# Retention's rotation moved from TensorE to copies within SBUF, in a stack of four mixed layers

## The reference, cut to what matters

```python
def _rotary(t, positions):
    half = t.shape[-1] // 2
    freq = ROPE_BASE ** (-jnp.arange(half, dtype=jnp.float32) / half)
    ang = positions.astype(jnp.float32)[..., None] * freq
    cos = jnp.cos(ang)[:, :, None, :]
    sin = jnp.sin(ang)[:, :, None, :]
    t1 = t[..., :half].astype(jnp.float32)
    t2 = t[..., half:].astype(jnp.float32)
    return jnp.concatenate([t1 * cos - t2 * sin, t1 * sin + t2 * cos], axis=-1).astype(t.dtype)
...
def _layer(x, c, positions, norm_g, w_ada, b_ada, w_in, conv_w, conv_b,
           dt_bias, a_log, d_skip, ssd_norm_g, b_forget, w_out):
...
    ret = _retention(rq.reshape(b, L, RET_HEADS, RET_HEAD_DIM),
                     rk.reshape(b, L, RET_HEADS, RET_HEAD_DIM),
                     rv.reshape(b, L, RET_HEADS, RET_HEAD_DIM), positions)
    ret = ret.reshape(b, L, RET_WIDTH) * jax.nn.silu(rg)
...
    mixed = jnp.concatenate([ret.astype(x.dtype), ssd.astype(x.dtype), fox.astype(x.dtype)], axis=-1)
    out = mixed @ w_out
    return x + gate[:, None, :] * out
```

## Time and profile before

| | us |
|---|---|
| median of 3 runs | 3217.77 (3216.93 to 3218.05) |
| the profiled execution: its own time | 3218.23 |
| its span | 3216.4 |
| TensorE busy | 3149.3 (98%) |
| VectorE busy | 1725.1 (54%) |
| ScalarE busy | 1205.2 (37%) |
| GpSimd busy | 446.8 (14%) |

### The profile page before, as it was taken

One profiled execution on the slowest core, in us unless ns is written; L12 is line 12 of the kernel. 1 busy time (PEld: TensorE's weight loads), 2 busy tenths in 40 slices (PEclk: granted clock), 3 DMA queues, 4 the chain that ended last, 5 costly groups with the idle time before them and its releaser, 6 DMA issues.

```text
span 3216.4 us, 43798 instructions
## 1 busy us (share of the span) xinstructions
PE 3149.3 (98%) x18127; PEld 2503.1 (78%) x18127; DVE 1725.1 (54%) x2545; ACT 1205.2 (37%) x1919; POOL 446.8 (14%) x359
## 2 busy tenths in 40 slices
PE   8999999999999999999999999999999999999999
PEld 6776778876777888887777788888888887778887
DVE  7965456845456443347877544345464334553333
ACT  4355434535542322233344432223352224342221
POOL 0022012003000310112322021011011001011110
PEclk9999999999999999999999999999999999999999
DMA  6764233336331233342100133333223322023332
GB/s 240 243 189 139 66 105 122 121 109 175 91 105 59 93 98 98 99 121 92 60 2 2 47 114 106 94 97 98 89 91 96 99 87 81 8 89 98 99 95 82
DMA packets 103654, 321.60 MB, mean 100 GB/s; under 512 B 10657, under 2 KB 26273, under 8 KB 101281
## 3 DMA queue, kind: packets, MB, share of 16 engines
q1 hardware_dynamic: 98128, 296.77, 29.8%
q10 hardware_dynamic: 5328, 22.02, 2.1%
HBM read 309.05 MB, written 9.70 MB: 99 GB/s over the span
## 4 chain that ended last, share of the span: by engine, by line
PE 86%; DVE 4%; ACT 2%; issue 1%; POOL 1%; DMA 0%; SPq 0%; DVEq 0%; POOLq 0%; ACTq 0%
PE acc L497 71%; PE acc L2553 1%; PE acc L1540 1%; PE acc L2539 1%; PE aux L1838 1%; PE aux L3334 1%; PE aux L1852 1%; PE acc L1865 1%; PE acc L2040 1%; PE aux L2029 1%; ACT w_hi L401 1%; PE aux L3339 1%; DVE ssd_ex L1429 0%; PE acc L3373 0%; DVE w_lo L408 0%
## 5 line engine op out<-in xcount | busy, mean ns | idle before, releaser
L497 PE MATMUL acc<-op_hi,w_hi 128*128 128x512 f32 x2624 | 1072.1, 409 | 7.4 <-DVE op_lo L1176 3.9
L401 ACT ACTIVATE w_hi<-raw 128x1024 fp32r<-128x1024 f32 (+2 forms) x476 | 494.1, 1038 | 1487.6 <-PE acc L497 1477.4
L497 PE MATMUL acc<-op_lo,w_hi 128*128 128x512 f32 x2624 | 1026.7, 391 | 0.0
L497 PE MATMUL acc<-op_hi,w_lo 128*128 128x512 f32 x2624 | 1026.3, 391 | 0.0
L408 DVE TENSOR_TENSOR w_lo<-raw,w_hi 128x1024 fp32r<-128x1024 f32 (+2 forms) x476 | 579.2, 1217 | 252.7 <-ACT w_hi L401 252.2
L497 PEld LDWEIGHTS acc<-op_hi,w_hi 128*128 128x128 f32 x2624 | 494.3, 188 | 136.8 <-issue 35.0
L497 PEld LDWEIGHTS acc<-op_lo,w_hi 128*128 128x128 f32 x2624 | 494.8, 189 | 106.2 <-issue 9.8
L497 PEld LDWEIGHTS acc<-op_hi,w_lo 128*128 128x128 f32 x2624 | 494.1, 188 | 105.3
L497 PE MATMUL acc<-ffn_hi,w_hi 128*128 128x512 f32 x800 | 311.8, 390 | 0.0
L497 PE MATMUL acc<-ffn_hi,w_lo 128*128 128x512 f32 x800 | 311.6, 390 | 0.0
L497 PE MATMUL acc<-ffn_lo,w_hi 128*128 128x512 f32 x800 | 311.6, 389 | 0.0
(11 more groups left out here) (592 smaller groups left out, 3574.2 us busy)
## 6 DMA issues: line engine op xcount, KB each, us to landing
raw<-in_w SPq DMA_DIRECT2D x436, 512.0 KB, 3.6
late_ada<-in_ada ACTq DMA_DIRECT2D x32, 512.0 KB, 4.5
raw<-in_w SPq DMA_DIRECT2D x32, 384.0 KB, 2.9
ssd_ex<-cum SPq DMA_DIRECT2D x16, 512.0 KB, 5.4
ssd_ex<-cum SPq DMA_DIRECT2D x16, 384.0 KB, 6.4
ada<-in_ada ACTq DMA_DIRECT2D x4, 1024.0 KB, 14.5
ada<-in_ada SPq DMA_DIRECT2D x4, 1024.0 KB, 21.8
ssd_ex<-cum SPq DMA_DIRECT2D x16, 256.0 KB, 4.8
```

The source lines that it names most:

```text
L401: act.activation(self.w_hi[g % AHEAD][:, 0:k, :], self.raw[s][:, 0:k, :], ACT.Copy).then_inc(self.split_hi.handle, 1)
L497: mm = pe.matmul(self.bank(s, g), w[:, k, :], a[:, k, 0:s.n], start=(k == 0 and q == 0), stop=(k == k_tiles - 1 and q == 2))
```

## The change

The product with `rot` is taken off TensorE. SyncE copies the two halves of the partitions of a tile, swapped, into one of four buffers (`swaps`, at the place of the forgetting attention's v, which is read by then). The sign goes into the sines: in the startup the sine's angle is multiplied by -1 on the lower half of the partitions (`half_sign`, in place of `rot` in the constant table). GpSimd multiplies the tile by the cosines in place, VectorE the swapped copy by the sines in place, and then adds the copy to the tile. The rotation no longer waits for the end of the forgetting attention, only for its transposes of v; its first copy is due 33 units before `start` (and no earlier than two units after the begin of retention's v pieces), the following ones 3.4 units apart. From the fifth copy on, a copy waits until the add has freed its buffer.

```diff
@@ -123,10 +123,7 @@
-    rot = np.zeros((P, P))
-    rot[i[:HD] + HD, i[:HD]] = -1.0
-    rot[i[:HD], i[:HD] + HD] = 1.0
-    parts["rot"] = rot
+    parts["half_sign"] = np.where(i < HD, -1.0, 1.0)[:, None]
@@ -970,7 +967,7 @@
-                act.activation(dst[:, :], dst[:, :], ACT.Sin).then_inc(*self.sined.inc())
+                act.activation(dst[:, :], dst[:, :], ACT.Sin, scale=1.0 if i else core.c("half_sign")).then_inc(*self.sined.inc())
@@ -1955,14 +1952,14 @@
-        self.part, self.part2 = core.place("ret_part", [P, 2, T], 8), core.place("ret_part2", [P, 2, T], 12)
...
-        self.swapped, self.cosed, self.sined, self.turned = (core.share("rot_" + s, n) for s in (
-            "swapped", "cos", "sin", "done"))
+        self.cosed, self.sined, self.turned = (core.share("rot_" + s, n) for s in ("cos", "sin", "done"))
+        self.swaps = core.place("ret_swap", [P, 4, T], 16.125)
+        self.swapped = [core.share(f"rot_swapped{i}", 32 * n // 4) for i in range(4)]
@@ -1983,7 +1980,7 @@
-        self.start, self.fox = start, fox
+        self.start, self.fox, self.first_swap = start, fox, max(linear.starts[first + 1] + 2.0, start - 33.0)
@@ -2003,21 +2000,21 @@
-        return (load(),)
+
+        def swaps():
+            for j in range(2 * RET_HEADS):
+                yield self.rotation(j)
+                if j == 0:
+                    sp.wait_ge(*self.qk_ready)
+                    sp.wait_ge(*self.fox.turn_v.done())
+                if j >= 4:
+                    sp.wait_ge(*self.turned.ge(j - 3))
+                for dst, src in ((slice(0, HD), slice(HD, P)), (slice(HD, P), slice(0, HD))):
+                    sp.dma_start(self.swaps[dst, j % 4, :], self.qk[src, j, :]).then_inc(*self.swapped[j % 4].inc(16))
+        return load(), swaps()
...
-        def rotations():
-            for j in range(2 * RET_HEADS):
-                yield self.start + 1.6 * j
-                if j == 0:
-                    pe.wait_ge(*self.qk_ready)
-                    pe.wait_ge(*self.fox.done())
-                if j >= 2:
-                    pe.wait_ge(*self.sined.ge(j - 1))
-                pe.matmul(core.aux[j % 2][:, :], core.c("rot"), qk[:, j, :], start=True,
-                          stop=True).then_inc(*self.swapped.inc())
...
+    def rotation(self, j):
+        return self.first_swap + 3.4 * j
@@ -2090,13 +2090,9 @@
-                yield self.start + 1.6 * j
-                if j == 0:
-                    pool.wait_ge(*self.qk_ready)
-                    pool.wait_ge(*self.fox.done())
-                if j >= 2:
-                    pool.wait_ge(*self.turned.ge(j - 1))
-                pool.tensor_tensor(self.part[:, j % 2, :], self.qk[:, j, :], self.core.cos[:, :],
+                yield self.rotation(j) + 5.0
+                pool.wait_ge(*self.swapped[j % 4].ge(32 * (j // 4 + 1)))
+                pool.tensor_tensor(self.qk[:, j, :], self.qk[:, j, :], self.core.cos[:, :],
                                    ALU.mult).then_inc(*self.cosed.inc())
@@ -2105,16 +2101,14 @@
-                yield self.start + 1.6 * j + 1.4
-                dve.wait_ge(*self.swapped.ge(j + 1))
-                if j >= 2:
-                    dve.wait_ge(*self.turned.ge(j - 1))
-                dve.tensor_tensor(self.part2[:, j % 2, :], core.aux[j % 2][:, :], core.sin[:, :],
-                                  ALU.mult).then_inc(*self.sined.inc())
+                yield self.rotation(j) + 5.0
+                dve.wait_ge(*self.swapped[j % 4].ge(32 * (j // 4 + 1)))
+                swap = self.swaps[:, j % 4, :]
+                dve.tensor_tensor(swap, swap, core.sin[:, :], ALU.mult).then_inc(*self.sined.inc())
+                yield self.rotation(j) + 6.8
                 dve.wait_ge(*self.sined.ge(j + 1))
                 dve.wait_ge(*self.cosed.ge(j + 1))
-                dve.tensor_tensor(qk[:, j, :], self.part[:, j % 2, :], self.part2[:, j % 2, :],
-                                  ALU.add).then_inc(*self.turned.inc())
+                dve.tensor_tensor(qk[:, j, :], qk[:, j, :], swap, ALU.add).then_inc(*self.turned.inc())
```

More of the change, by code:

```diff
@@ L2063, in spreads @@
                 mm.then_inc(*self.spread.inc())
-        return rotations(), scores(), values(), means(), spreads()
+        return scores(), values(), means(), spreads()
     def norm_time(self, h):
         return self.norms + 6.8 * h
+    def rotation(self, j):
+        return self.first_swap + 3.4 * j
     def act(self, act):
```

## The result

The kernel after the change took 3224.62 us (median, 3221.59 to 3226.89), the kernel before on the same chip 3216.78 (3214.76 to 3219.19): ratio 1.0024, 95% interval 1.0016 to 1.0031. It is 7.8 us slower, 0.24%; the forecast was no change (+0.6 us). On the forecast's scale, where before is 3217.77, that is 3225.6: inside the range, near the end that Rival B set.

The account below looks back on a forecast made before the run. TensorE, busy 98% of the span, was taken to bound the kernel. Two layers of 8.7 us removed, 8.5 given back waiting and 0.5 for the clock made +0.6 us: 3218.4, range 3205 to 3227.

Parts of the forecast that it names:

- Rival B: Copies land 1.9 us later than taken, holding VectorE's third and sixth sine products and then TensorE: 3227 us; chance 0.16.
- main case: TensorE's saved time is given back waiting for low halves at the first output piece: +0.6 us, 3213 to 3226; chance 0.6.
- Removed: 8.7 us a layer: On TensorE, eight rotations with their waits, between the first rotation and retention's scores, go: 8.7 us a layer, 17.4 in all.
- VectorE waits for GpSimd: VectorE instructions with two SBUF inputs wait for GpSimd's cosines to finish: an add takes 1.27 us instead of 0.69.
- The sign that was named: In the new profile, adds and sine products mostly take above 0.69 us where a GpSimd cosine overlaps.
- The wait for a copy: VectorE's third and sixth sine products wait 1.2 and 1.3 us for copies landing 3.9 after the weight load's issue.
- w(g0) done at 418.0: VectorE's weight split after the first of four gate pieces, begun at 416.74, ends at 418.0, its cosines being over earlier.
- The clock: 0.5 us: After TensorE's 5.1 us pause at the first output piece, the lower granted clock costs 0.5 us a layer, possibly 0 to 2.1.
- From there to the scores: After the first output piece, TensorE's 11 triples and four transposes take 9.6 us, as now; scores at 455.3.
- The sum: Two layers of 8.7 us removed, 8.5 given back waiting for low halves and 0.5 for the clock: +0.6 us.
- Rival A: Cosines stay out of VectorE's way, so TensorE's first scores start at 449.2: 6.3 us a layer gained, 3205; chance 0.24.

Follow-up runs that it names:

- the run in which nothing is waited for: Rotation arithmetic due 10 units earlier and copies 18 than in the changed kernel; 3199.08 us with cosines on VectorE, 3199.99 on GpSimd, against 3216.63 and 3217.04 before.

## Where the prediction was right and where it was wrong, point by point

The time came out inside the stated range, but the sum said no change, and 7.8 us were lost: mainly one term of it was too small. The main case's own range, 3213 to 3226, holds the time as well, and that is luck: its upper end is made of a clock term that cost nothing and of a landing at most 1.1 us late.

- *Removed: 8.7 us a layer.* Right: 8.92 by the count of the run in which nothing is waited for.
- *VectorE waits for GpSimd.* Right, and a cost as large as that of the copies (13.6 us without cosines, 12.6 without the waits). From the start of m2 to the end of lo7 are 24.66 us; without the wait of 2.82 before m5, 21.84, where the working has 8.5 and 13.3, 21.8. The sign that was named, sine products above 0.69 as well, did not show in the changed kernel: in its first layer none of them met a cosine that had begun before it. Where one did, it took 1.78 (the row of 418.94 above), so the add of 1.27 was the right nearest row, not the sine product from PSUM. The Trainium skill's rule of the exclusive port pair (SBUF — State Buffer, "SBUF: two separate sides") agrees: the split takes 2.30 beside cosines and 1.22 without.
- *The wait for a copy: the step that failed.* Copies 2 and 5 were taken to land 3.9 us after the load's issue, "just behind that load, since one queue carries both". They landed 5.64 and 5.48 after in the first layer, 5.53 and 5.28 in the second: 1.74, 1.58, 1.63 and 1.38 too late, 6.3 us in all. Even the upper bound, 5.0, was too low. The working let the copy land 0.3 us behind a load of 3.6; it came some 2 us behind one of 3.5 (the median), and the 16 DMA engines were busy for 0.87 or more of each us from 421 to 424. With no load ahead its landing is 2.4, near the lower bound's 2.0.
- *w(g0) done at 418.0.* 1.0 us late in the first layer and 0.5 in the second, counted from the attention's last add: copies 0 and 1, behind a weight load themselves, landed up to 5.0 us after their issue, in the first layer at 415.1, and their cosines still ran over w(g0).
- *The clock: 0.5 us.* It was granted 1.00 until 436, then 0.50 to 0.52 for the rest of the pause and some 5 us of work behind it, longer than I thought, and cost nothing: TensorE still had to wait for a low half at 448.43 (0.30 us), and first scores come 10.3 us after the last low half, both in the changed kernel (449.04 to 459.30) and after the much shorter pause with the copies earlier (439.3 to 449.6); the working had 10.4.
- *From there to the scores: 9.6 after o0.* Right, by the same numbers.
- *The sum.* 1.0 and 0.5 for w(g0) and 6.3 for the landings, less 1.0 for the clock: 6.9 over the forecast of +0.6, 7.5. The count lost 4.1 us in the first layer (45.53 against 41.40) and 3.3 in the second (937.73 to 982.42 against 41.40), 7.4 in all; the medians say 7.8.
- *The rivals.* What came is Rival B: it had the place, m2 and m5, the price, 4 us for each us of landing, and the sign, m2 after 423.4 (424.38), right. The landing was 1.58 late on average, just over its deciding 1.5; the 1 to 2 us for the clock in its price did not come, and w(g0) took their place. Its 0.16 was too little. Its ground, a weight load ahead of copies 2 and 5, was in the rows; against it I set the landings of two other transfers (2.0 and 3.2), without reading what stood ahead of those. Rival A's condition did not come about. The run without cosines meets half of it and gains 5.8 us over before; A's own time, 3205, stays untested for this placement.

## What to carry to other kernels

A transfer's price depends on what is in flight with it. On one queue, put a small copy that an engine waits for ahead of the large prefetch that nobody waits for yet (2.4 us against 4.2 here), and take most of the load ahead as added to its landing. Beside a 2 MB load on another queue, a place ahead of it did not help (12.0). When work is moved off the bounding engine, follow the engine that receives it to the next thing that the bounding engine wants from it (here the low halves), and move the work to where that engine idles; copies and arithmetic need leads of their own. Two engines that share a port do not halve the work unless the second runs in the first one's pauses: 1.28 us on GpSimd cost VectorE 0.9, which could have done it in 0.6.

## What the runs showed that I had not expected

- A copy of one half of a tile within SBUF (128 KB, 64 partitions) holds SyncE 0.6 us at its issue, where a 512 KB load holds it 0.33.
- Its landing is 2.4 us (2.2 at best), 4.2 with a 512 KB load issued just ahead, 10.5 behind a 2 MB load on the same queue and up to 12.0 beside one on another queue. Whether those are the load alone was not tried.
- The scaled probabilities that TensorE waits for under the attention are late even with GpSimd idle (2.16 us with the cosines on VectorE), so it is the list of VectorE, and not only the shared port, that holds them.
